# Taking the low-rank maps of the RWKV-7 recurrence two at a time, on the two row halves of the TensorE array

## What is computed

```python
lora_w = jnp.einsum('ebtr,erd->ebtd', jnp.tanh(jnp.einsum('btd,edr->ebtr', xw, w1)), w2)
decay = _heads(jnp.exp(-jnp.exp(-jax.nn.softplus(-(w0[:, None, None, :] + lora_w).astype(f32)) - 0.5)))
lora_a = jnp.einsum('ebtr,erd->ebtd', jnp.einsum('btd,edr->ebtr', xa, a1), a2)
a = _heads(jax.nn.sigmoid((a0[:, None, None, :] + lora_a).astype(f32)))
k_dir = k[None] * (1.0 + (a - 1.0) * _heads(k_a))
# one step of the scan, for each direction e and each head
S = S * w_t[:, :, None, :] + sa[..., None] * (kk_t * a_t)[:, :, None, :] + v_t[..., None] * k_t[:, :, None, :]
y_t = jnp.einsum('bhvk,bhk->bhv', S, r_t)
```

## Time and profile before

| | |
|---|---|
| median of 3 runs | 2433.33 us (2431.37 to 2438.89) |
| the profiled execution, its own time | 2441.6 us |
| its span in the profile | 2439.6 us |
| granted TensorE clock over the span, as a share | 0.937 |
| recurrence, its stretch in the span | about 397 to 1067 us |
| busy: PE, PEld, DVE, ACT, POOL | 88%, 72%, 45%, 35%, 20% of the span |

### The profile page before, as it was taken

The page is one execution under the profiler, slowest core; times in us unless marked ns, Lnnn a source line. Parts: engine busy times, 40 slices in busy tenths (PEclk is TensorE's granted clock), DMA queues, the critical chain, the costliest instruction groups (busy, mean ns, idle before and its releaser), DMA issues. The chain is left out here.

```text
span 2439.6 us, 60964 instructions
## 1 busy us (share of the span) xinstructions
PE 2142.7 (88%) x26707; PEld 1756.9 (72%) x26707; DVE 1099.3 (45%) x1506; ACT 866.0 (35%) x1426; POOL 487.5 (20%) x348
## 2 busy tenths in 40 slices
PE   5899997678778888759899999999897978999998
PEld 4586685566767777648788888888774547788887
DVE  3633322666777667532422222222357544333333
ACT  3223223455565556431333112221333543431231
POOL 0313222654665456301000000001121001000000
PEclk8698998798999989989899999999898998999999
DMA  9566754001100110032222212222120012333332
GB/s 316 176 191 188 222 169 127 10 20 32 32 22 15 31 32 11 4 119 69 61 69 60 71 50 69 60 70 60 44 61 9 0 35 69 89 104 92 95 108 82
DMA packets 262162, 191.78 MB, mean 79 GB/s; under 512 B 11946, under 2 KB 252468, under 8 KB 261428
## 3 DMA queue, kind: packets, MB, share of 16 engines
q1 hardware_dynamic: 261940, 188.45, 25.6%
HBM read 170.60 MB, written 17.83 MB: 77 GB/s over the span
## 5 line engine op out<-in xcount | busy, mean ns | idle before, releaser
L520 DVE TENSOR_TENSOR ffn_lo<-ffn_raw,ffn_hi 128x1024 fp32r<-128x1024 f32 (+1 forms) x120 | 159.8, 1332 | 547.3 <-ACT ffn_hi L515 547.3
L527 PE MATMUL banks<-operand_hi,ffn_hi 128*128 128x512 f32 (+1 forms) x1056 | 377.1, 357 | 15.3 <-DVE operand_lo L486 12.2
L528 PE MATMUL banks<-operand_lo,ffn_hi 128*128 128x512 f32 (+1 forms) x1056 | 377.7, 358 | 0.0
L529 PE MATMUL banks<-operand_hi,ffn_lo 128*128 128x512 f32 (+1 forms) x1056 | 374.7, 355 | 0.0
L515 ACT CAST ffn_hi<-ffn_raw 128x1024 fp32r<-128x1024 f32 (+1 forms) x120 | 136.3, 1136 | 508.8 <-PE banks L529 507.6
L527 PEld LDWEIGHTS banks<-operand_hi,ffn_hi 128*128 128x128 f32 x1056 | 200.4, 190 | 46.8 <-DVE operand_lo L486 12.8
L1770 POOL TENSOR_TENSOR lvl<-sc_b,level_mask 128x512 f32<-128x512 f32 x144 | 192.4, 1351 | 206.2 <-DVE sc_b L1544 124.8
L529 PEld LDWEIGHTS banks<-operand_hi,ffn_lo 128*128 128x128 f32 x1056 | 199.7, 189 | 30.0
L528 PEld LDWEIGHTS banks<-operand_lo,ffn_hi 128*128 128x128 f32 x1056 | 200.2, 190 | 27.8
L528 PE MATMUL banks<-ffn_g_lo,ffn_hi 128*128 128x512 f32 (+1 forms) x528 | 188.0, 356 | 0.0
L527 PE MATMUL banks<-ffn_g_hi,ffn_hi 128*128 128x512 f32 (+1 forms) x528 | 187.4, 355 | 0.0
(11 more groups left out here) (246 smaller groups left out, 4701.5 us busy)
## 6 DMA issues: line engine op xcount, KB each, us to landing
mod_raw<-in_mod_w SPq DMA_DIRECT2D x96, 512.0 KB, 6.2
ffn_raw<-in_ff_w SPq DMA_DIRECT2D x88, 512.0 KB, 3.9
ffn_raw<-in_ff_w SPq DMA_DIRECT2D x32, 704.0 KB, 4.7
proj_raw<-in_rw_wr SPq DMA_DIRECT2D x8, 512.0 KB, 5.2
proj_raw<-in_rw_wk SPq DMA_DIRECT2D x8, 512.0 KB, 4.8
proj_raw<-in_rw_wv SPq DMA_DIRECT2D x8, 512.0 KB, 5.2
rwkv_out_raw<-in_rw_wo SPq DMA_DIRECT2D x8, 512.0 KB, 4.1
qk_w_raw<-in_at_wq SPq DMA_DIRECT2D x8, 512.0 KB, 4.1
```

The lines of the kernel that those rows point to most:

```text
L520: signal(eng, eng.tensor_tensor(self.lo[s][:, 0:k_tiles, :], self.raw[s][:, 0:k_tiles, :], self.hi[s][:, 0:k_tiles, :].bitcast(F32), ALU.s ...
L527: pe.matmul(out, w[0], x[0], start=first, stop=False)
L528: pe.matmul(out, w[0], x[1], start=False, stop=False)
L529: return pe.matmul(out, w[1], x[0], start=False, stop=last)
```

## The change

The four maps become two calls, and each call computes both directions of one kind: for each stretch of tokens, one matmul on the upper 64 rows into one work bank, and one on the lower 64 rows into the other. `map0` and `map2` keep their places in the count of work-bank uses and issue nothing. `map1` and `map3` wait for both banks and then issue all eight records. The calls and the sigmoids move in the list: the decay pair with both its sigmoids stands behind `u_copy(C, 0)`, the gate pair stands behind `t_copy(A, 1)`, its sigmoids behind `swap(B, 4)`.

```diff
@@ -1068,7 +1068,7 @@
                 if part == 0:
                     behind("y_sum")
                 if part == 1:
-                    ahead("map0")
+                    ahead("map0", "map1", "sigmoid0", "sigmoid1")
                 products(C, 0, following(0))
                 if part == 0:
                     ahead("r_decay1")
@@ -1086,8 +1086,6 @@
                 cut(A, 0)
                 if part == 0:
                     ahead("r_decay0")
-                if part == 1:
-                    ahead("sigmoid0")
                 if part == 2:
                     ahead("bonus_product", "growth1")
                 t(B, 3)
@@ -1133,15 +1131,15 @@
                 if part == 2:
                     ahead("b_gate1")
                 flip(B, 4)
+                t_copy(A, 1)
                 if part == 1:
-                    ahead("map1")
-                t_copy(A, 1)
+                    ahead("map2", "map3")
                 swap(B, 4)
                 if part == 0:
                     behind("y_scale")
                 cut(A, 2)
                 if part == 1:
-                    ahead("sigmoid1", "map2", "scan1", "sigmoid2")
+                    ahead("scan1", "sigmoid2", "sigmoid3")
                 if part == 2:
                     ahead("through0")
                 products(C, 2, following(2))
@@ -1150,11 +1148,7 @@
                     ahead("key_gate0")
                 values_copy(A)
                 update(C, 2)
-                if part == 1:
-                    ahead("map3")
                 y(A, 1)
-                if part == 1:
-                    ahead("sigmoid3")
                 if part == 2:
                     ahead("k_grow0")
                 rhs(C, 3, following(3))
@@ -1207,8 +1201,8 @@
                 for name in names:
                     feature(0, name)
 
-            first("kk_square", "kk_sum", "kk_limit", "map0", "sigmoid0", "scan0", "map1", "sigmoid1", "scan1",
-                  "map2", "sigmoid2", "key_gate0", "k_gate0", "map3", "sigmoid3", "key_gate1", "k_gate1",
+            first("kk_square", "kk_sum", "kk_limit", "map0", "map1", "sigmoid0", "scan0", "sigmoid1", "scan1",
+                  "map2", "map3", "sigmoid2", "key_gate0", "k_gate0", "sigmoid3", "key_gate1", "k_gate1",
                   "k_sum", "kk_root", "kk_invert", "kk_spread", "kk_scale", "through0", "growth0", "b_gate0", "a_decay0", "k_grow0",
                   "r_decay0", "through1", "growth1", "b_gate1", "b_grow0", "a_decay1", "k_grow1", "r_decay1", "b_grow1",
                   "bonus_product", "bonus_sum", "bonus")
@@ -1493,16 +1487,22 @@
                     def feature(self, t, name):
                         if engine_of(name) != "pe":
                             return
+                        if name in ("map0", "map2"):
+                            return
                         bank = self.work_free("side", t, name)
                         if name == "kk_sum":
                             after(pe, self.use, t, "kk_square")
                             mm = self.sum_tokens(bank, tmp)
-                        elif name in ("map0", "map1", "map2", "map3"):
-                            m = int(name[3])
+                        elif name in ("map1", "map3"):
+                            m = int(name[3]) // 2
+                            banks = (self.work_free("side", t, f"map{2 * m}"), bank)
                             pe.wait_ge(*sliced(t))
                             for at, width in SEGS:
-                                mm = pe.matmul(tokens_of(bank)[:, at:at + width], lora_w[t % 2][half(m % 2), m // 2, :],
-                                               hidden[half(m % 2), m // 2, at:at + width], start=True, stop=True)
+                                for h in range(2):
+                                    mm = pe.matmul(tokens_of(banks[h])[:, at:at + width], lora_w[t % 2][half(h), m, :],
+                                                   hidden[half(h), m, at:at + width], start=True, stop=True)
+                                    if at and h == 0:
+                                        mm.then_inc(features["pe"], 1)
                         elif name == "kk_spread":
                             after(pe, self.use, t, "kk_invert")
                             mm = self.spread(bank, norm_k)
```

## The result

The changed kernel took 2433.12 us (median of 22 runs, 2422.46 to 2443.37), the kernel before 2425.24 (22 runs, 2418.59 to 2438.89). The ratio is 1.0028, with a 95% interval of 1.0015 to 1.0041: slower by 6.8 us, between 3.6 and 10.0 (the two medians lie 7.9 apart). That is less than the 0.3% I had called the bound of what can be told, so by that yardstick it is the "same" that I gave 0.34, though with 22 runs each the sign is clear. The forecast difference was +9.0 us and lies inside the interval. The forecast time, 2442, is 9 us too high, since the three runs that I started from (2433.33) lay 8 us above the median of 22. The measured time lies outside the forecast's own range, 2438 to 2448, and inside the wide one, 2426 to 2457.

What follows compares the result with a forecast made beforehand. The prediction took slots to grow with TensorE's work, with ScalarE late next. It summed 6.3 us for seven slots and 2.7 for the start to +9.0, from a 2433.33 baseline: 2442 us, own range 2438 to 2448, wide range 2426 to 2457.

Steps and rivals of the forecast that it cites:

- table loads more, in the slots: ScalarE in the slots: the order sigmoid, root, sigmoid needs 12 more table loads, of 1.28 us each.
- `t_copy(B, 3)` late: First half of slot 7: ScalarE copies `t(B, 3)` only after swap, root load and root, 2.6 us late.
- `t(B, 4)` late: TensorE in slot 7: lateness carried from the first half into the second, 1.1 us, with ends 0 and 2.3.
- `values` late beyond that: Second half of slot 7: `values` waits for `sigmoid2`, starting at 687.6 for 686.50, carried lateness left aside.
- `kk_spread` late: Second half of slot 7: `kk_spread` waits for `values_copy` on ScalarE; slot 7 ends about 1.2 us later.
- pair 0's start: Ahead of the slots: pair 0's bare chain waits for ScalarE, 2.7 us slower, bounds 1 and 3.5.
- it moves by 1.0 only and takes the rest in: TensorE's idle stop ahead of `t(B, 4)` shifts by 1.0 us and absorbs the remaining first-half lateness, leaving 1.1 us.
- their stretch grows by 5 to 8: Sign of being right: the slots' stretch grows by 5 to 8 us while TensorE's work there falls by 15.
- All taken in by the stops: Rival: TensorE's idle stops absorb the slots' delay, leaving a mean of 0.2 us a slot; 2437.5 us, chance 0.24.
- TensorE paces: Rival: TensorE's work sets the slot's length, so each slot gains 1.5 us; 2425.5 us, chance 0.14.
- No overlap: Rival: the row halves do not run beside each other, so each pair takes 3.1 us; 2466 us, chance 0.03.
- The clock falls: Rival: new TensorE waits lower the granted clock, costing each slot another 1.7 us; 2454 us, chance 0.17.

Runs made afterwards that it cites:

- e2: The kernel before with only pair 0's maps paired, ahead of the slots; 2437.47 us, ratio 1.0025 to the kernel before.
- e9: The kernel before with two redundant TensorE semaphore waits fewer per pair; 2433.78 us, ratio 1.0000 to the kernel before.
- e3: The changed kernel with pair 0's start as before, so the change in the slots alone; 2433.73 us, ratio 1.0003 to the kernel before.
- a2: The changed kernel run once more, unaltered, for a second profile; 2437.08 us, ratio 1.0024 to the kernel before.
- e10: The changed kernel with two redundant TensorE waits per pair put back; 2443.68 us, ratio 1.0019 to the kernel before.
- e8: The kernel before with each map over all 128 rows, summing both directions and so changing the output; 2428.72 us, ratio 0.9998 to the kernel before.
- e1: The changed kernel with the decay sigmoids moved behind `swap(B, 2)` and `kk_root`; 2434.09 us, ratio 1.0011 to the kernel before.
- e4: The kernel before with only `kk_root` moved behind `sigmoid0`, no maps paired; 2435.48 us, ratio 1.0018 to the kernel before.
- e11: The kernel before with `map1` and `sigmoid1` ahead of `t(B, 4)`, only gate maps paired, `values_copy` ahead of `key_gate0`; 2426.24 us, ratio 0.9989.

## Why the prediction was right or wrong

**What held.** The sign, the size of the difference, and the mechanism of the two row halves, the table loads and the late copy. By its own steps, in slot 7, lateness being against before's rows less 5.81 us:

| step | forecast | measured |
|---|---|---|
| a pair of maps at full clock | 1.6 us | 1.56 |
| a pair at the low clock, ahead of the slots | 3.0 | 2.93 |
| table loads more, in the slots | 12 | 12 |
| `score(A, 1)`, held by the first sigmoid, starts at | 674.25 | 674.19 (668.38 + 5.81) |
| `t_copy(B, 3)` late | 2.6 | 2.3 |
| `y(B, 3)` late | 2.3 | 2.1 |
| `t(B, 4)` late | 1.1 | 2.3 |
| `values` late beyond that | 1.1 | 0.8 |
| `kk_spread` late | 1.2 | 1.9 |
| pair 0's start | 2.7 | 2.64 |

**What failed** are two terms that were mis-sized. The one that misses the time is the baseline of the sum, "The median of the runs shown is 2433.33": over 22 runs it is 2425.24, 8.1 less. Set against that, 2442 would be 16.8 us slower, where 6.8 was measured.

**The step of the walk that failed** is the sentence "it moves by 1.0 only and takes the rest in". I let the stop ahead of `t(B, 4)` swallow half of the first half's lateness. It did not: TensorE idles there for 1.43 us again (1.35 in the earlier trace rows; this time ahead of the last of `products(C, 1)`), all the same late, and `t(B, 4)` starts 2.3 us behind. The second half then gave 0.4 back (`kk_spread` is 1.9 late). Slot 7 lost 1.9 where I had 1.2. But slot 7 is a single one at full clock. The six slots with maps from slot 1 on sum to 166.0, 159.9 and 164.9 us in the profiles with before's order of them (before, e2, e9) and to 169.9, 169.3, 166.5 and 172.4 in those with the change's (after, e3, a2, e10): 5.9 more in the mean, with a standard error of 2.2 from the scatter of these seven profiles, or 1.0 a slot. The seventh, slot −2, shows no carried lateness: from the slots' first score mask to slot 0's it is 45.2 us before and 43.2 after, with 17 us at the lower clock in both. Some 6 us for the slots, where I had 6.3: slot 7 lost more than I gave it, slot −2 less, and these cancel, which is luck.

This sum is of the slots with maps alone. The other slots were shorter in three of the four profiles with the change's order, at less time on the lower clock. So of the sign "their stretch grows by 5 to 8" nothing shows in the first profile: there the stretch fell by 13 us and TensorE's work by 19. The times give the slots' part as +5.1 ± 1.2 at equal clock and as a ratio of 1.0003 plain (e3).

Two smaller slips: the four maps of a pair of heads still update their semaphore four times, twice in each call, so no updates are saved; and the copy of `t(B, 3)` started 0.76 us behind `t(B, 3)` already before, not 0.2, and 2.09 behind it after.

**The rivals.** "All taken in by the stops" falls with the same row; in slot 7 the first half's stop took in nothing. "TensorE paces" falls too: its work on maps fell by 13 us in the slots (40.48 to 27.23 by the windows of the map line, some of it clock), and the slots with maps grew. "No overlap" falls with 1.56. "The clock falls" had the wrong sign. The mean clock of the change's kernels is not below before's (.9411 for .9403 and .9405 for .9386; e3 .9434 for .9401), and the windows show 0.95 for 0.93. At 1.18 us per 0.001 this is worth 1 to 4 us in the change's favour; it is what lies between e3's 1.0003 plain and its +5.1 at equal clock. What raises it was not separated. In e8 a higher clock went with more rows at work, and the pair has both halves at work at once, but for less time.

**The rule on table sets.** The Trainium skill, ScalarE: Activation LUTs, section "Table sets: the hidden batching unit", was right to speak against this order: e1, which has the loads of before, is 3.1 to 4.9 us faster than the change at equal clock, and e4, which moves the root alone and so adds 12 loads, 6.0 slower than the kernel before. The same page of the Trainium skill, in "What ACT_TABLE_LOAD costs", prices a switch at 2.66 us with its drain, and this trace does not agree: the root's load starts 0.02 us behind the swap's end (669.14 + 0.82 to 669.98) and takes 1.28, and the root follows 0.02 later.

**The absolute number.** The forecast missed by 9 us for a reason outside its argument: a median of three runs, of a kernel whose runs scatter by 5 us, was taken as the baseline. With that scatter such a baseline has a standard error of some 3 us, and before's medians of five other sittings lie between 2427 and 2437, so a forecast of the absolute time is no better than that. The wide range had room for it, the forecast's own range had not.

**What stays open.** Why the clock is higher in the changed order; how much of e11's 3 us is real, and whether the pair brings it; and what the remaining 0.92 us of e1's late copy is worth, since the third work bank that would remove it was not tried.

## What to carry to other kernels

When two products are made at the same time, count what they take together: two output banks at once, and two readers in a row ahead of everything that comes next on the reading engine. Here pairing cost time where it dragged a load and a root in between (the decay pair); where the readers had the table loaded and nothing short queued behind them (the gate pair of e11), it cost nothing that shows and may have paid. Put the tiny instruction with the other table first, and check it by the count of loads. Do not let an idle stretch called "issue" absorb a delay in a forecast.

## What the runs showed of the hardware

- **Two row halves overlap almost perfectly**: eight records in 1.56 us where four take 1.55, with two output banks, in 8 of the 9 pairs of the changed kernel's slots that ran at full clock throughout (the ninth took 2.24).
- **The time of a run goes with its granted clock**, 1.18 us for 0.001, with the same kernel. Taking that out removes half of the variance, which helps where differences are of 0.2%. In 4 of the 12 comparisons (e1, e3, e8, e11) the plain interval holds 1 and the figure at equal clock is over two standard errors from nothing.
- **A fuller array went with a higher clock.** e8's matmuls are as many, as wide and as long as before's, over 128 rows for 64; its 12 runs have .9471 for .9403. Of the two levels, 2.4 and 1.2 GHz, the lower one held for 51 us of the slots in place of 85 in its single profile. It also lost the overlap of `map1` and `map2`, so its maps keep TensorE at work for longer at full clock, and which of the two the clock went with was not separated. The time was no better for it (0.9998).
- **TensorE's stops at "issue" stayed unexplained.** The page of the changed kernel lists a queue of instructions, with packets of some 16 KB (3.03 MB in 185), and between 670 and 685 us it brought three of them. That the stops hang on the place of an instruction in this stream is argued only: with two waits a pair fewer, e9's stops in the six slots with maps sum to 14.1 us where before's are 11.0, and e10's to 19.0 where the change's are 19.2, and neither time moved beyond its error. In the changed order 1.66 us a slot of this is the wait ahead of `y(B, 3)`, if the other slots are as slot 7. The queue's line:

```profile
q8 instruction: 185, 3.03, 0.5%
```
